# GpSimd's weight remainders in a recurrent mixer, paced by the decay levels that VectorE merges

## The reference

```python
log_f = jnp.logaddexp(jnp.log(lbf), jnp.log1p(-lbf) + jax.nn.log_sigmoid(ff))
k = (1.0 - lbf) * jax.nn.sigmoid(-ff)
q = jax.nn.silu(q.astype(f32))
...
def step(state, inp):
    qc, kc, vc, gc = inp
    b = jnp.cumsum(gc, axis=2)
    o_inter = jnp.einsum('bhtk,bhkv->bhtv', qc * jnp.exp(b), state)
    diff = b[:, :, :, None, :] - b[:, :, None, :, :]
    decay = jnp.exp(jnp.where(causal[:, :, None], diff, -jnp.inf))
    a = jnp.einsum('bhtk,bhsk,bhtsk->bhts', qc, kc, decay)
    o_intra = jnp.einsum('bhts,bhsv->bhtv', a, vc)
    ...
    return new_state, o_inter + o_intra
```

## Time and profile before

| | |
|---|---|
| median of 3 runs | 1949.17 us (1949.12 to 1950.05) |
| profiled execution, its own time | 1950.58 us |
| span in that profile | 1948.8 us |
| TensorE busy | 1928.0 us (99% of the span) |
| VectorE busy | 1084.5 us (56%) |
| ScalarE busy | 633.4 us (32%) |
| GpSimd busy | 898.8 us (46%) |
| recurrent mixer | about 1296 to 1575 us of the span |

### The profile page before, as it was taken

The page is one execution under the profiler, slowest core; times in us unless marked ns, Lnnn a source line. Parts: engine busy times, 40 slices in busy tenths (PEclk is TensorE's granted clock), DMA queues, the critical chain, the costliest instruction groups (busy, mean ns, idle before and its releaser), DMA issues.

```text
span 1948.8 us, 26135 instructions
## 1 busy us (share of the span) xinstructions
PE 1928.0 (99%) x10793; PEld 1633.9 (84%) x10793; DVE 1084.5 (56%) x1620; ACT 633.4 (32%) x789; POOL 898.8 (46%) x596
## 2 busy tenths in 40 slices
PE   8999999999999999999999999999999999999997
PEld 8888888978788888888988888889988988888886
DVE  2755473555373665653465647265544675546655
ACT  3333232264423233322333323232233123323321
POOL 4453555533324455445445446444433345355544
PEclk9999999999999999999999999999999999999999
DMA  6232322321204333232423232322222222332321
GB/s 235 92 106 87 130 87 87 106 74 66 66 23 152 109 107 108 65 108 87 152 87 108 65 129 87 108 87 88 69 84 66 66 77 97 108 128 89 108 66 44
DMA packets 135590, 185.45 MB, mean 95 GB/s; under 512 B 3360, under 2 KB 119088, under 8 KB 135472
## 3 DMA queue, kind: packets, MB, share of 16 engines
q1 hardware_dynamic: 135312, 183.53, 28.5%
q10 hardware_dynamic: 160, 0.26, 0.1%
HBM read 181.42 MB, written 2.10 MB: 94 GB/s over the span
## 4 chain that ended last, share of the span: by engine, by line
PE 97%; DVE 2%; DMA 1%; ACT 0%; issue 0%; SPq 0%; POOL 0%; DVEq 0%; ACTq 0%
PE psum L1506 31%; PE psum L1507 30%; PE psum L1508 30%; PE psum L1816 2%; PE psum L1757 1%; PE psum L1530 1%; PE psum L1789 1%; PE psum L1770 1%; DMA raw<-in_ffn_w 1%; PE psum L1844 0%; PE psum L1847 0%; PE psum L1834 0%; DVE xt_lo L1015 0%; DVE arena L1212 0%; ACT w_hi L757 0%
## 5 line engine op out<-in xcount | busy, mean ns | idle before, releaser
L694 POOL TENSOR_TENSOR w_lo<-raw,w_hi 128x512 fp32r<-128x512 f32 x524 | 848.8, 1652 | 922.4 <-ACT w_hi L757 897.8
L1506 PE MATMUL psum<-xt_hi,w_hi 128*128 128x512 f32 (+1 forms) x1824 | 675.0, 370 | 2.2 <-DVE w_lo L1372 0.9
L1507 PE MATMUL psum<-xt_lo,w_hi 128*128 128x512 f32 (+1 forms) x1824 | 670.8, 368 | 0.0
L1508 PE MATMUL psum<-xt_hi,w_lo 128*128 128x512 f32 (+1 forms) x1824 | 670.7, 368 | 0.0
L1506 PEld LDWEIGHTS psum<-xt_hi,w_hi 128*128 128x128 f32 x1824 | 343.8, 188 | 65.3 <-issue 4.5
L1508 PEld LDWEIGHTS psum<-xt_hi,w_lo 128*128 128x128 f32 x1824 | 343.8, 189 | 57.1
L1507 PEld LDWEIGHTS psum<-xt_lo,w_hi 128*128 128x128 f32 x1824 | 343.9, 189 | 55.9
L757 ACT ACTIVATE w_hi<-raw 128x2048 fp32r<-128x2048 f32 x132 | 251.7, 1911 | 345.4 <-PE psum L1508 343.5
L1076 DVE SCALAR_TENSOR_TENSOR x<-psum,x 128x512 f32<-128x512 f32 x224 | 145.6, 684 | 131.5 <-PE psum L1508 128.3
L771 ACT ACTIVATE gate<-psum 128x512 f32<-128x512 f32 x88 | 52.5, 598 | 307.9 <-PE psum L1508 307.9
L1506 PE MATMUL psum<-w_hi,xt_hi 128*128 128x256 f32 (+2 forms) x448 | 139.8, 312 | 0.0
(11 more groups left out here) (178 smaller groups left out, 2147.1 us busy)
## 6 DMA issues: line engine op xcount, KB each, us to landing
raw<-in_ffn_w SPq DMA_DIRECT2D x115, 1024.0 KB, 5.4
raw_odd<-in_ffn_w SPq DMA_DIRECT2D x16, 1024.0 KB, 5.1
raw<-in_hgrn_w_in SPq DMA_DIRECT2D x16, 1024.0 KB, 5.5
raw<-in_attn_w_in SPq DMA_DIRECT2D x9, 1024.0 KB, 6.2
raw<-in_attn_w_out SPq DMA_DIRECT2D x4, 1024.0 KB, 4.9
raw<-in_hgrn_w_out SPq DMA_DIRECT2D x4, 1024.0 KB, 5.0
lng<-in_ln_g SPq DMA_DIRECT2D x6, 512.0 KB, 4.3
lnb<-in_ln_b SPq DMA_DIRECT2D x6, 512.0 KB, 5.4
```

The costliest lines, as they stand in the source:

```text
L694: op = pool.tensor_tensor(w_lo[:, slot_of[s], cols], raw[:, slot_of[s], cols], w_hi[:, slot_of[s], cols].bitcast(F32), ALU.subtract)
L1506: pe.matmul(out_, w[0], xs[0], start=first, stop=False)
L1507: pe.matmul(out_, w[0], xs[1], start=False, stop=False)
L1508: return pe.matmul(out_, w[1], xs[0], start=False, stop=last)
```

## The change

`low(s)` gets a list of at most four values of `level_merged`. Before its piece number i, GpSimd waits for value number i of the list, if there is one. `levels_ahead` makes the list from the schedule: the levels (a = 0 left out) that stand behind the step at which GpSimd has this `low`, up to the slab's own first quarter or the next `outputs` step, whichever is first, and of these the first four. No arithmetic is changed, and no instruction but the waits is added. In the attention mixer there are no levels, and the feed-forward networks and the first two calls of a mixer don't pass a list.

```diff
+def levels_ahead(plan, at, s):
+
+    ends = [i for i, step in enumerate(plan) if i > at and (step == ("quarter", s, 0) or step[0] == "outputs")]
+    ahead = plan[at + 1:ends[0]] if ends else []
+    return [7 * step[1] + step[2] for step in ahead if step[0] == "level" and step[2]][:4]
...
-            def low(s):
+            def low(s, merged=()):
 
                 pool.wait_ge(hi_ready, s + 1)
                 for part in range(4):
+                    if part < len(merged):
+                        pool.wait_ge(level_merged, merged[part])
                     cols = slice(part * SLAB // 4, (part + 1) * SLAB // 4)
...
-                                low(s0 + s)
+                                low(s0 + s, levels_ahead(plan, at, s))
```

## The result

The changed kernel takes 1955.07 us (median of 10 runs, 1954.2 to 1955.9), against 1949.51 us for the kernel before (10 runs, 1949.12 to 1950.22). The ratio is 1.0027 with a 95% interval of 1.0019 to 1.0036, so it is slower by 5.6 us. The forecast was 1952.5 us; the case that came about is the one with a chance of 0.14, in which the clock falls in the stall. It was said to take 1954.5 to 1956.5 us. The stated range was 1951.3 to 1955.0 us. The median lies 0.07 us above its end, and the rise of 5.6 us within the 5.8 us that its end allows above 1949.17 us, from which it was counted.

A forecast was written before the change was run, and what follows sets the result against it. TensorE, busy 99% of the span, was taken as the bound. A 3.96 us stall at slab 8 less 0.65 us gained gave 3.3 us more, from 1949.17 to 1952.5 us; bounds 1952.0 to 1954.1, range 1951.3 to 1955.0 us.

The forecast's parts named there:

- the clock's case: Rival, chance 0.14: the clock falls in slab 8's stall, costing about 2 to 4 us more, 1954.5 to 1956.5 us.
- the prediction's own signs: Wrong if TensorE waits at other slabs, the clock is down behind the stall, or slab 8's fourth piece isn't awaited.
- The stall: Before slab 8's first quarter: its fourth piece waits for level (1,4), so TensorE stalls 3.96 us.
- slab 13 with its 0.16 us: Slab 13's fourth piece, waiting for level (2,4), ends 0.16 us before TensorE's need; taken as no cost, up to 0.3 us possible.
- no load came late: SyncE's slab loads, held up behind the waits, have room: no load, nor ScalarE instruction behind one, becomes late.
- the pause is shorter than the one after which it fell: Argument against the clock falling at slab 8: a 3.9 us pause, against some 4.1 us at the span's end.
- eight transposes in 2.10 us: At the span's start, after 3.91 us without work, eight transposes take 2.10 us, against 1.09 us in the mixer.
- the forecast's sum: Whole kernel: 3.96 us of stall less 0.65 us gained, 3.3 us more.
- What is given back: Group 3, fewer GpSimd and VectorE collisions: 0.67 + 0.41 - 0.43 = 0.65 us gained, bounds nothing and 1.08 us.
- The 0.67 us before level (3,4): TensorE's loss before level (3,4), from a collision in level (3,3), goes: 0.67 us won.
- the gain before the turned keys: TensorE's loss before the keys of group 3 are turned goes: 0.41 us won.
- The catching up of slab 18: Slab 18's first three pieces follow late slab 17 into level (3,5), making TensorE wait about 0.43 us.

The follow-up runs named there:

- The first two experiments: Changed kernel without slab 8's fourth wait: 1949.28 us, ratio 0.9999; kernel before plus only that wait: 1955.79 us, ratio 1.0031.
- the shortest stall: Changed kernel, slab 8's fourth piece waiting for level (1,4)'s scaling, its pieces 640, 640, 640 and 128 columns: 1952.97 us, 3.4 us above before.
- All four profiles with an idle pause of 2.9 us or more: Changed kernel 1955.07 us, the one wait alone 1955.79 us, changed kernel with stall altered to 2.9 us 1954.42 us and to 5.2 us 1956.34 us.
- the single execution of 1952.92 us: The kernel of the shortest stall, unchanged, run again for one profiled execution: 1952.92 us.
- the other single execution: The kernel of the shortest stall, unchanged, run once more for one profiled execution: 1954.1 us.
- the one wait alone: Kernel before, with only slab 8's fourth piece waiting for level (1,4): 1955.79 us, ratio 1.0031.

## Why the prediction was wrong in its mechanism and close in its number

The measured rise lies at the very end of the stated range, and that is luck. The forecast's own account reached to 1954.1 us, and the range went on to 1955.0 only to take in the lower end of the clock's case. By the prediction's own signs it is wrong, since the clock is down behind the stall. It also gave 0.62 to a difference within 0.2%, 3.9 us, and 0.36 to a slower kernel; 5.6 us are beyond that line.

**The stall, right.** Slab 8's fourth piece behind level (1,4) was put at 3.96 us and measured 3.95 us, at the place and with the releaser that were named. The first two experiments show that this one wait is the whole loss. No other slab stalled TensorE, slab 13 with its 0.16 us included, and no load came late.

**The clock, the step that failed.** The case was there as a rival, with 0.14, because "the pause is shorter than the one after which it fell" at the end of the span. That read the earlier trace rows as a threshold. One fall 4.1 us after the last work (4.0 us by the 0.90 of the earlier trace rows, which puts it at 1942.8) shows that a pause of that length can bring the clock down, not that a shorter one can't. In the changed kernel it fell some 2.2 us into the pause; with the shortest stall it fell though the pause was only 2.0 us. All four profiles with an idle pause of 2.9 us or more show the half clock, and two of the three with 2.0 us. The price was given as 2 to 4 us, from how long TensorE "stayed at 1.2 GHz". It measured 1.4 to 2.8 us. In the changed kernel the half clock lasted 6.9 us, nearly twice the pause, but 1.7 us of it lie in the pause, where there is nothing to slow; the rest cost 2.35 us. The row that the price was taken from, eight transposes in 2.10 us at the start of the span, does not show the clock as its cause: the profile gives the granted clock there as 1.00. With the clock kept up by transposes in the stall, the time is 3.9 us above before, where the forecast's sum was 3.3 us. So the term that failed is the clock's: the forecast put it at nothing, and it is worth 1.7 us by the medians and 2.35 us in the profile.

**What is given back, smaller than thought.** The term was 0.65 us and measured 0.24 us in the profile. The 0.67 us before level (3,4) were won as said (0.66), and the gain before the turned keys too (0.50 for 0.41). The catching up of slab 18 cost more: VectorE's two multiplies collide in level (3,5), and again in (3,6), so TensorE waits twice, 0.25 and 0.43 us, where one wait of 0.43 us was expected. The 0.25 us before (2,7) were not in the sum. There slab 14's first three pieces collide with the multiplies of (2,5) and hold up that level's merge to 1488.18. Slab 14's fourth piece and slab 15's first wait for this merge, and they meet another instruction of VectorE, L1193, which makes a head's decays for group 3. It takes 1.30 us where it took 0.55 us before, as L1184, and the multiplies of (2,6), queued behind it, end late:

```profile
1488.25 2.52 POOL L703 TENSOR_TENSOR w_lo<-raw,w_hi 128x512 fp32r<-128x512 f32 x2 [1.05 <-DVE arena L1236]
```
```profile
1489.76 1.30 DVE L1193 TENSOR_SCALAR arena<-gate,span,lower 128x512 f32<-128x512 f32 x1 [1.58 <-ACT hid L862]
```
```profile
1484.61 0.55 DVE L1184 TENSOR_SCALAR arena<-gate,span,lower 128x512 f32<-128x512 f32 x1 [4.45 <-ACT hid L853]
```

VectorE's timeline of the changed kernel shows the multiplies of levels (3,5) and (3,6) beside the pieces of slab 18, the longer ones being those that collide:

```profile
1541.07 1.37 DVE L1220 TENSOR_TENSOR arena<-arena 128x512 f32<-128x512 f32 x1 [1.78 <-PE psum L1825]
1542.37 1.78 DVE L1221 TENSOR_TENSOR arena<-arena 128x512 f32<-128x512 f32 x1
...
1546.91 1.79 DVE L1221 TENSOR_TENSOR arena<-arena 128x512 f32<-128x512 f32 x1
```

So a wait that spreads a slab's pieces also pushes the next slab into the levels. The experiment with waits at slabs 18 and 19 alone wins the full 1.15 us, since nothing queues up behind them.

**The sum after the fact.** 3.95 + 2.35 - 0.24 = 6.06 us in the profile, 5.6 us between the medians. The spread of the clock's price, 1.4 us in one profile of a 3.95 us stall and 2.35 us in another, is larger than that difference.

## What to carry to other kernels

When a wait is added to a helper engine, look for the consumer: here 41 waits together cost nothing, and one did, because the level that it waited for stood directly ahead of the use. A list of such waits should end a step or two before the use. Where TensorE is the bound, price a pause of two microseconds or more as the pause plus a possible spell at half clock, which cost 1.4 to 2.8 us here. If the pause can't be avoided, give TensorE something harmless to do in it: the transposes won back 1.7 us. And pace only the work that collides on the critical path: five waits, at slabs 18 and 19, won 1.2 us, where the 41 free ones of the change together won nothing that the times show.

## What the runs showed of the hardware that was not expected

The clock can fall after TensorE has gone back to work. In the single execution of 1952.92 us the pause ended at 1405.33. The clock went down about a microsecond later, as the products, 0.23 us apart at first, show by their lengths:

```profile
1405.33 0.47 PE L1519 MATMUL psum<-w_hi,h_hi 128*128 128x512 f32 x1 [2.04 <-issue]
...
1406.10 0.39 PE L1519 MATMUL psum<-w_hi,h_hi 128*128 128x512 f32 x1
1406.33 0.54 PE L1520 MATMUL psum<-w_lo,h_hi 128*128 128x512 f32 x1
1406.67 0.63 PE L1521 MATMUL psum<-w_hi,h_lo 128*128 128x512 f32 x1
```

So the same pause costs 2.1 us in one execution and 3.7 us in the next. In the other single execution the clock fell at 1407.8, 1.4 us after the pause. How long the clock stays down differs too: in the six profiles with a fall it was at half for 3.4 us in three (both single executions and the one wait alone) and for 6.8 to 6.9 us in the others. The Trainium skill, page "TensorE: Matmul & The Clock Gate", section "Why this matters for your kernels", advises against long idle gaps between bursts of matmuls, and the fall in the 3.95 us pause agrees. The pause of 2.04 us is shorter than the gaps that the page warns of, and the clock fell in two profiles of three; there the measurement decides. What makes the clock fall in one execution and not in the next stays open. Every pause here also stands behind a level of small products, and no run shows whether the same pause among full products would do it.

Transposes of the identity, which the stall was filled with, were enough to keep the clock at 1.00 in the profiles of both kernels that had them.
